# Loading the even layer's input weights by column groups in order of use, with a narrower router product, in a two-layer diffusion backbone

## The reference, cut to what matters

```
def modulate(x, g, shift, scale):
    return rms_norm(x, g) * (1.0 + scale) + shift

# even layer, context tokens and latent tokens alike
h = modulate(x, g_mix, shift, scale)        # shift, scale from silu(c) @ w_ada + b_ada
qa, ka, va, qk_b, vb, ob, gates = split_cols(h @ w_in, (512, 128, 128, 1024, 512, 512, 16))

# channel mixer of every layer
scores = sigmoid(tokens @ w_router)         # (T, 1024) @ (1024, 32)
```

## Time and profile before

| | |
|---|---|
| median of 3 runs | 3671.84 us (3670.82 to 3674.42) |
| the profiled execution | 3682.23 us |
| its span, first to last instruction | 3680.4 us |
| mean granted TensorE clock | 0.937 |
| PE busy | 3254.6 us (88%), 17427 instructions |
| DVE, ACT, POOL busy | 1454.0, 833.2, 255.9 us |
| bytes moved by DMA | 676.90 MB, mean 184 GB/s |

### The profile page before, as it was taken

The page is one execution under the profiler, slowest core; times in us unless marked ns, Lnnn a source line. Parts: engine busy times, 40 slices in busy tenths (PEclk is TensorE's granted clock), DMA queues, the critical chain, the costliest instruction groups (busy, mean ns, idle before and its releaser), DMA issues. The chain is left out here.

```text
span 3680.4 us, 48549 instructions
## 1 busy us (share of the span) xinstructions
PE 3254.6 (88%) x17427; PEld 1784.0 (48%) x17428; DVE 1454.0 (40%) x4226; ACT 833.2 (23%) x1602; POOL 255.9 (7%) x321
## 2 busy tenths in 40 slices
PE   5999966789999779999998799899999869999983
PEld 2776733754445434444444355477775534444431
DVE  2333353655555521111111588666665431111114
ACT  1111112355531100000000344355552100000000
POOL 0000002500023000000000000000002000000001
PEclk7999977899999889999999899899999979999997
DMA  9600058400032169999884422200003157799998
GB/s 349 248 23 23 12 226 281 120 9 1 1 105 98 46 246 384 381 384 364 310 320 175 144 86 86 75 1 1 1 1 122 63 206 302 299 361 377 401 411 314
DMA packets 280201, 676.90 MB, mean 184 GB/s; under 512 B 23044, under 2 KB 35508, under 8 KB 278964
## 3 DMA queue, kind: packets, MB, share of 16 engines
q1 hardware_dynamic: 249300, 559.07, 40.4%
q0 software_dynamic: 20176, 76.55, 5.7%
q10 hardware_dynamic: 10512, 38.28, 2.6%
HBM read 579.32 MB, written 94.50 MB: 183 GB/s over the span
## 5 line engine op out<-in xcount | busy, mean ns | idle before, releaser
L2570 PE MATMUL ex_ps_g<-w_ring,ex_xT 128*64 128x512 f32 x1696 | 396.9, 622 | 54.1 <-issue 50.9
L2601 PE MATMUL ps_y<-w_ring,ex_hT 128*64 128x512 f32 x1696 | 399.0, 602 | 0.0
L2582 PE MATMUL ps_u<-w_ring,ex_xT 128*64 128x256 f32 x3392 | 389.7, 382 | 8.9 <-DMA w_ring<-in_w 8.9
L2582 PEld LDWEIGHTS ps_u<-w_ring,ex_xT 128*64 128x64 f32 x3392 | 243.8, 137 | 153.1 <-issue 39.3
L2570 PEld LDWEIGHTS ex_ps_g<-w_ring,ex_xT 128*64 128x64 f32 x1696 | 127.4, 143 | 294.6 <-issue 291.6
L1657 PE MATMUL of_ps_r<-of_w,cat 128*128 128x512 f32 (+1 forms) x608 | 257.7, 580 | 3.0 <-ACT cat L1740 3.0
L401 PE MATMUL ps_r<-w,hT 128*128 128x512 f32 (+1 forms) x640 | 248.2, 544 | 1.5 <-ACT hT L465 1.5
L2666 DVE SCALAR_TENSOR_TENSOR ex_hr<-ex_th,ex_ps_g 128x512 f32<-128x512 f32 x53 | 36.4, 688 | 441.6 <-ACT ex_th L2644 441.6
L2601 PEld LDWEIGHTS ps_y<-w_ring,ex_hT 128*64 128x64 f32 x1696 | 107.6, 136 | 178.1 <-issue 178.1
L1382 PE MATMUL mo_ps_o<-mo_w,mo_cT 128*128 128x512 f32 x416 | 184.6, 596 | 1.0 <-DMA mo_w<-in_e_w_out 0.5
L2111 DVE TENSOR_SCALAR_CACHE_REDUCE oa_sx<-oa_ps_s 128x512 f32<-128x512 f32 (+1 forms) x288 | 160.2, 598 | 58.3 <-PE oa_ps_s L2027 57.2
(11 more groups left out here) (486 smaller groups left out, 4408.6 us busy)
## 6 DMA issues: line engine op xcount, KB each, us to landing
w_ring<-in_w SPq DMA_DIRECT2D x768, 512.0 KB, 10.6
ml_staging<-in_w_ada SPq DMA_DIRECT2D x14, 2048.0 KB, 12.3
y_dram<-zeros POOLq DMA_DIRECT2D x2, 14080.0 KB, 66.1
y_dram<-ex_y ACTq DMA_DIRECT2D x53, 512.0 KB, 6.3
ml_spare<-in_w_ada SPq DMA_DIRECT2D x6, 2048.0 KB, 12.7
w<-in_e_w_in SPq DMA_DIRECT2D x8, 1416.0 KB, 20.6
ml_arena<-ml_rows SPq DMA_DIRECT2D x40, 256.0 KB, 4.3
f_dram<-mo_f SPq DMA_DIRECT2D x18, 512.0 KB, 2.9
```

The source lines that it names most:

```text
L2570: mm = pe.matmul(ps_g[rows, :], xT[:, k, rows], weight(k // 2)[:, h, (k % 2) * DE:(k % 2 + 1) * DE], start=k == 0, stop=k == KD - 1)
L2582: mm = pe.matmul(ps_u[rows, f, 0:256], xT[:, k, rows], weight(4 + k // 2)[:, h, at:at + 256], start=k == 0, stop=k == KD - 1)
L2601: mm = pe.matmul(ps_y[rows, half, :], hT[:, k, rows], weight(8 + k)[:, h, half * 512:(half + 1) * 512], start=k == 0, stop=k == 3)
```

## The change

Five edits:

- The columns of `w` in SBUF get a new order: queries, keys and values (0 to 767), gates (768 to 783), `qk_b` (`W_Z`, 784 on), `vb` and `ob` (`W_V`, 1808 on). Four transfers, one for each column group over all 1024 rows, replace the eight; they are issued as queries/keys/values, gates, `vb`/`ob`, `qk_b`, on three semaphores.
- PE waits for the first two groups ahead of row group 0 of the first tile, for the third ahead of row group 2, for the fourth ahead of `channels`; nothing waits ahead of the transposes. POOL's zero fill waits for the last transfer, as before.
- Row group 1 is one product 272 columns wide (keys, values, gates) in place of a 256-column and a 128-column one.
- The first two token tiles are issued by SP in the first block, between the last `w_ada` piece and the broadcasts, no longer by ACT at the start of the second block.
- `wr` is 32 columns wide, is not cleared, and is loaded without a wait; the router's product moves 32 columns.

```
+W_QKV, W_GATES, W_Z, W_V = 0, AW + 2 * AKW, AW + 2 * AKW + 4 * BH, AW + 2 * AKW + 4 * BH + 2 * BW
+W_COLUMNS = ((W_QKV, (0, AW + 2 * AKW), 0), (W_GATES, (IN_EVEN - 4 * BH, IN_EVEN), 0),
+             (W_V, (AW + 2 * AKW + 2 * BW, IN_EVEN - 4 * BH), 1), (W_Z, (AW + 2 * AKW, AW + 2 * AKW + 2 * BW), 2))
...
+                for h in range(2):
+                    sp.dma_start(L.x[:, h, :], A["ctx"][0, h * P:(h + 1) * P, :]).then_inc(L.x_in[h], 16)
...
-                for k in range(KD):
-                    sp.dma_start(L.w[:, k, :], A["e_w_in"][0, k * P:(k + 1) * P, :]).then_inc(L.w_in, 16)
+                for at, (a, b), group in W_COLUMNS:
+                    sp.dma_start(L.w[:, :, at:at + b - a], A["e_w_in"][0, :, a:b].rearrange("(k p) n -> p k n", p=P)).then_inc(L.w_in[group], 16)
...
-                pool.wait_ge(L.w_in, 16 * KD)
+                pool.wait_ge(L.w_in[2], 16)
...
+                        if place_of(i, h)[0] and n in (0, 2):
+                            pe.wait_ge(L.w_in[n // 2], (32, 16)[n // 2])
...
-                        if n == 1:
-                            for k in range(KD):
-                                mm = pe.matmul(ps_r[:, n, 256:384], hT[:, h, k, :], w[:, k, IN_EVEN - P:IN_EVEN],
-                                               start=k == 0, stop=k == KD - 1)
...
+                    if place_of(i, h)[0]:
+                        pe.wait_ge(L.w_in[2], 16)
...
-                pe.wait_ge(L.w_in, 16 * KD)
...
-                for h in range(2):
-                    act.dma_start(x[:, h, :], A["ctx"][0, h * P:(h + 1) * P, :]).then_inc(x_in[h], 16)
...
-                    dve.tensor_tensor(L.gates[:, bass.ds(i * 2 + h, 1), :], ps_r[:, 1, 3 * P - 4 * BH:3 * P].unsqueeze(1),
+                    dve.tensor_tensor(L.gates[:, bass.ds(i * 2 + h, 1), :], ps_r[:, 1, 2 * AKW:2 * AKW + 4 * BH].unsqueeze(1),
...
-        wr = nc.alloc_sbuf_tensor(tag + "wr", [P, KD, P], F32)
+        wr = nc.alloc_sbuf_tensor(tag + "wr", [P, KD, NE], F32)
...
-                sp.wait_ge(wr_clear, 1)
-                sp.dma_start(wr[:, :, 0:NE], A["w_router"].rearrange("(k p) e -> p k e", p=P)).then_inc(r_in, 16)
+                sp.dma_start(wr[:, :, :], A["w_router"].rearrange("(k p) e -> p k e", p=P)).then_inc(r_in, 16)
...
-                        mm = pe.matmul(ps_r[:, 0:P], fT[:, k, :], wr[:, k, :], start=k == 0, stop=k == KD - 1)
+                        mm = pe.matmul(ps_r[:, 0:NE], fT[:, k, :], wr[:, k, :], start=k == 0, stop=k == KD - 1)
...
-                dve.memset(wr[:, :, :], 0.0).then_inc(wr_clear, 1)
```

More of the change, by code:

```diff
@@ L316, in even_project @@
     QK = AW + AKW
-    Z0 = AW + 2 * AKW
-    V0 = Z0 + 2 * BW
+    Z0, V0 = W_Z, W_V
     with nc.cleanup_on_exit():
-        w = L.w
-        x = nc.alloc_sbuf_tensor("x", [P, 2, D], F32)
+        w, x = L.w, L.x
         hT = nc.alloc_sbuf_tensor("hT", [P, 2, KD, P], F32)
@@ L343, in even_project @@
         x_sq, xh_ready = s("x_sq"), s("xh_ready")
-        x_in = [s("x_in0"), s("x_in1")]
+        x_in = L.x_in
         t_done, h_act, h_dve = s("t_done"), s("h_act"), s("h_dve")
@@ L1281, in mix_out @@
         gate_in = [s("gate_in0"), s("gate_in1")]
-        r_in, wr_clear, row_mm, row_out = s("r_in"), s("wr_clear"), s("row_mm"), s("row_out")
+        r_in, row_mm, row_out = s("r_in"), s("row_mm"), s("row_out")
         x_in, x_st = [s(f"x_in{b}") for b in range(4)], [s(f"x_st{b}") for b in range(4)]
@@ L2814, in build @@
             L.w = nc.alloc_sbuf_tensor("w", [P, KD, IN_EVEN], F32)
-            L.w_in = nc.alloc_semaphore("e_w_in_loaded")
+            L.w_in = [nc.alloc_semaphore(f"e_w_in_loaded{n}") for n in range(3)]
+            L.x = nc.alloc_sbuf_tensor("x", [P, 2, D], F32)
+            L.x_in = [nc.alloc_semaphore(f"ep_x_in{h}") for h in range(2)]
             modulation(nc, g, A, L)
```

## The result

| | before | after |
|---|---|---|
| median of 5 runs each, measured together | 3674.42 us (3670.82 to 3678.6) | 3657.01 us (3645.97 to 3665.19) |
| ratio of the times, 95% interval | | 0.995, 0.9928 to 0.9972 |
| the profiled execution, its span | 3682.23, 3680.4 | 3665.19, 3663.4 |
| mean granted clock | 0.937 | 0.931 |
| PE busy, instructions | 3254.6 us, 17427 | 3246.3 us, 17267 |

The kernel is 0.5% faster: 17 us, where 31.3 were forecast, and 3657.0 lies outside the range of 3631 to 3649.

The account below looks back on a forecast made before the run. The even layer's input projection was taken as PE-bound, its start waiting for weights; start 13.5, gates' product 15.7, router 1.2 and clearing 0.9 sum to 31.3 us, taking the median from 3671.84 to 3640.5 us, range 3631 to 3649.

Parts of the forecast that it names:

- The start: Even layer's input projection: first row product at 53.6 instead of 66.31 us, with less time at half clock, saving 13.5 us.
- SP's hold: End of first block: SP's last issue ends only at 42.8 us, so the second block starts at 43.6, 6.3 us later than unheld.
- The clock: First tile: full clock granted 9.2 us after the first transpose, at 57.6; 0.85 us less lost at half speed.
- The column groups: Transfers of `w`: queries/keys/values land at 42.4 us, gates 43.2, `vb`/`ob` 53.7, `qk_b` 64.2, without delaying PE.
- The gates' 64-byte pieces: Gates' transfer of 1024 small pieces: taken as 0.8 us, between 0.1 for bytes alone and 1.5.
- The gates' product: Input projection, ten tiles: the wider product saves 1.57 us a tile, 15.7 us in all; bounds 8 to 17.8.
- some 1700 outstanding row pieces: SP's issues in the first block: a limit on outstanding pieces, not bytes, inferred from three issues, delays the last issue's end.
- Router product: Output projection's router: loads of the stationary side set the pace, so 32 columns save 0.004 us an instruction, 1.2 us.
- Clearing of `wr`: Ahead of the output projection's first tile: dropping DVE's clearing saves 0.9 us in the odd layer, nothing in the even.
- a later block takes longer than before: One of the listed signs that the forecast is wrong, for blocks behind the input projection; no size given.
- the forecast's other rivals: SP not held, 3634 us (0.15); little from the start, 3650 (0.13); router pays by columns, 3617 to 3640 (0.06); slower (0.02).

Follow-up runs that it names:

- the run without the hold: Changed kernel with the `vb`/`ob` and `qk_b` transfers issued at the start of the second block instead of the end of the first: 3642.55 us, ratio 0.9907.
- the kernel before, moved: Kernel before plus 66 counting instructions on PE at the mLSTM's start, putting the experts' loops where the changed kernel has them: 3684.94 us, ratio 1.0032.
- the changed one, moved back: Changed kernel plus 190 counting instructions on PE ahead of the experts: 3658.27 us in one place, 3642.86 us spread over four.
- half-way: Changed kernel plus 95 counting instructions on PE, experts' loops at a third position: 3613.02 us; kernel before with 161, same position: 3652.79 us.
- the repeated run: The changed kernel with 95 counting instructions on PE, same program run once more: 3615.98 us, ratio 0.9839.
- start undone: Changed kernel, but PE waits for all column groups before its first transpose and ACT loads the first two token tiles in the second block: 3664.41 us, ratio 0.9974.

## Why the prediction was wrong

**Right, by its own steps.** The start: SP's hold, its end (41.91 for 42.8), the first row product (52.82 for 53.6) and the gain of 13.5 us; undone, it costs 14.8 where it happens. The clock came back 10.0 us after the first transpose, near the 9.2 assumed. The column groups landed as summed: in the run without the hold at 42.1, 42.8, 54.3 and 64.5 for 42.4, 43.2, 53.7 and 64.2. The gates' 64-byte pieces took 0.7 us there, and 0.6 to 2.3 in the other runs, where 0.8 was forecast and bytes alone would give 0.16: they cost more than their bytes, but nothing waited for them. The gates' product: 1.50 us a tile for 1.57. Together they were to bring `channels` forward by 29.2 less what differs in the first tile, and it was 29.5.

One figure behind the hold was right by luck in part. The prediction put the limit at some 1700 outstanding row pieces, from the times at which PE was released. Counted from the DMA packets of the traces, 1470 to 1520 pieces of the earlier transfers were outstanding at the ends of its three issues; in the changed kernel it was 1629, 1316, 1340 and 1025 at the ends of the four of `w`. So pieces hold the issue and not bytes, but not at one number, and 1700 can't be carried elsewhere.

**Small terms.** Router product: 1.2 forecast, 0 measured in the time from the output projection to the experts (240.1 against 240.2). The size was right, 0.08 us a group where 0.07 was forecast, but the next group of the output projection takes 3.68 us in place of 3.60, so nothing of it reaches the chain. Clearing of `wr`: forecast 0.9 in the odd layer and nothing in the even one. From PE's first broadcast of the output projection (L1238) to its first product it took 12.9 us before and 12.1 after in the odd layer, 13.6 and 12.6 in the even one, so both gain, and the even layer's nothing was wrong by 1.0. Each is below what runs of the whole can tell.

**The step that failed** is the sum: 13.5 + 15.7 + 1.2 + 0.9 has terms for the stages that the diff touches and none for those behind them, so it put the change of the experts at nothing without a reason. The sentence under the streams, that nothing else on PE changed its place, is true of the order and not of where the code lies. The prediction did name "a later block takes longer than before" as a sign of being wrong, but priced nothing by it. Removing 80 products was costed as 1.57 us a tile. It also took some 190 instructions out of PE's program and so moved the code of all loops behind it. In the experts, where the weights' transfers fill the DMA engines, that costs 7 us in the even layer and 10 to 16 in the odd one, of which some 5 come back at the end (74 to 78 us after the experts for 78 to 83), for a reason that was not looked for. By the means it is 11 us (the kernel before, moved) or 9 to 10 (the changed one, moved back). Of the forecast's other rivals none took place.

**The account.** 3675.1, the mean of before over all its executions, less 31 for the parts, plus 9 to 11 for the placement, makes 3653 to 3655; measured are 3652.3, 3653.3 and 3655.8 in three sets. The median of 3671.84 from which I subtracted was from 3 executions, and 3 us low; the result's own median lies 4 to 5 us above the means of the later ones. Both pushed against the forecast: 3640.5 would have been 3644 from the better base, and 3643 is what the change gives with the loops in place.

**What is shown and what is argued.** Shown: counting instructions alone, in either kernel, change the number and length of the gaps and the time: 11 us slower at the changed kernel's position, 9 to 10 faster at that of before, 21 and 37 to 40 faster half-way, and the repeated run agrees. Transfers of instructions start with the gaps. Argued: that PE waits there for its own code, which a full set of DMA engines delivers late. The Trainium skill (Runtime: NRT & Kernel Launch, Instruction fetch mechanics) describes such a path: instructions come in blocks of 16 KiB, 256 of them, the fetch ahead is sequential, and a jump out of what is held stalls until the target arrives. The traces agree with the size of a transfer (2.57 MB in 157) and with gaps at the outer loop's jumps back, all of which pause. The Trainium skill (the same page and section) also calls the cost of crossing a boundary "mostly hidden", and the trace agrees for most of the 41 transfers a stage of the half-way run, which no gap goes with; the jumps are where it costs, up to 14.6 us for one and 32 to 74 us for all of them in the experts. Still open: which positions are good for which loop. Only three were tried, all three with two loops moved together. Why some of the other boundaries pause and some don't, and why the third jump back of the odd layer costs twice the others, was not settled.

## What to carry to other kernels

Where a kernel has loops, taking instructions away or adding them ahead of a loop is two changes: the one meant, and a move of all code behind it. Look at the gaps at "issue" in later loops with busy DMA, before crediting or blaming the edit. Counting instructions at places where the engine waits anyway, here 66 to 190 at 0.16 us each, undo the move, and trying two or three positions can be worth more than the edit. When a transfer is cut into more row pieces, count the pieces that its queue has outstanding, and don't leave the last of them to be issued ahead of a barrier. And with a spread of 7 us from one execution to the next, three are no base for a forecast to a tenth of a percent.

## What the runs showed of the hardware

- SP's issue of a transfer is held by the row pieces outstanding: four issues of 1024 pieces take 17.32 us, eight of 128 pieces with the same bytes 8.74. Behind the ends of held issues 1003 to 1629 pieces of earlier transfers were outstanding, and 480 once (start undone), so there is no one number. With two of the issues moved behind the barrier they take 7.98 us in the first block and 6.75 in the second, and the barrier opens at 35.1.
- The same loop, instruction for instruction, takes 601 to 628 us (odd layer's experts) by where its code lies. With nearly every gap the clock falls to its lower level, inside the gap or up to 1.3 us behind its end, and stays there until 2.7 to 6.1 us behind the end, so a gap costs more than its length.
- 16 float32 instructions with 32 moving columns take 1.97 us, with 128 columns 2.05, each with a new stationary side: a quarter of the columns saves next to nothing.
- A PE instruction that only adds to a semaphore takes 0.16 us (190 of them in 31.2 us).
